# One stage of a two-block transformer kernel reordered: half-column inverse updates, branch tiles and preparation steps moved, beta and roots partly on ScalarE

## The chip, the cores and the metric

The program runs on one core of one Trainium2 chip. The metric is the device time of the whole program in microseconds. TensorE multiplies matrices into PSUM, VectorE and ScalarE work elementwise (ScalarE also evaluates functions), GpSimd (POOL) works elementwise on SBUF alone, and SyncE issues the loads.

## The reference

Two transformer blocks on 512 tokens of width 1024. The second block adds 16 meta tokens (528 tokens) and mixes them with two branches, a gated delta net and a stick-breaking attention. The change lies in the delta net:

```python
q = l2norm(heads(jax.nn.silu(causal_depthwise_conv(dq, conv_q)), DN_DK))
k = l2norm(heads(jax.nn.silu(causal_depthwise_conv(dk, conv_k)), DN_DK))
v = heads(jax.nn.silu(causal_depthwise_conv(dv, conv_v)), DN_DV)
g = -jnp.exp(a_log) * jax.nn.softplus(da + dt_bias)
beta = jax.nn.sigmoid(db)
...
decay = jnp.exp(jnp.where(incl, g[..., :, None] - g[..., None, :], -jnp.inf))
lower = jnp.where(strict, jnp.einsum('nbhid,nbhjd->nbhij', kb, k) * decay, 0.0)
sol = lax.linalg.triangular_solve(eye + lower, rhs, left_side=True, lower=True)
...
v_new = u_c - jnp.einsum('bhcd,bhde->bhce', w_c, S)
o = jnp.einsum('bhcd,bhde->bhce', qd_c, S) + jnp.einsum('bhij,bhje->bhie', attn_c, v_new)
S = S * gl_c[..., None, None] + jnp.einsum('bhcd,bhce->bhde', kd_c, v_new)
...
o_dn = rmsnorm_2(o_dn, dn_gain) * jax.nn.silu(heads(dz, DN_DV))
merged = jax.nn.sigmoid(gate_dn) * (o_dn @ w_branch_dn) + ...
```

There are 8 heads, keys of 128 and values of 256 channels.

## The kernel before, in words

**Tiles.** Activations lie with channels on partitions and tokens along the columns. Each weight product is taken in three parts for precision (`quantum`, line 950): high weights by high activations, high by low, low by high, as fp32r matmuls at L965. A unit is 128 output channels, 8 quanta (the eight 128-channel pieces of the input), so 24 matmuls of 512 columns or 48 of 264. ScalarE makes the high part of a unit's weights (w_hi), VectorE or GpSimd the low part (w_lo), some units ahead.

**The delta net's stage.** Its order is written out by hand. `delta_order` (line 106) builds one list, DELTA, and all engines walk it, each taking its own share of each event. The list has fills (w_proj quanta, "mm", and quanta of the output branch, "branch") and steps. `merged` (line 79) puts a step ahead of the fill whose index its number has reached; steps with equal numbers keep the order in which they were added, the preparation (PREPARE) ahead of the scan (SCAN). After an opening of 80 quanta (heads 0 and 1 are projected, head 0 is prepared) pass i does, at once:
- 48 quanta: q, k and the two v units of head i+2 (slots of 264 x 2 columns) and the two z units of head i+1 (512 columns);
- 8 branch tiles of head i-1 (L1345, 6 matmuls of 512 columns), one after every second quantum of a unit (`beside`); pass 0 has none;
- PREPARE for head i+1: `bcast` (broadcast of gate and beta), `decay`, `pair` (kk and kq products, L1224), `turn` (a transpose, L1233), then the six levels x1, u1, ... x6, u6 of the inverse of a 128x128 triangular block, with four blocks of 128 and one of 16 (WIDE);
- SCAN for head i: v (L1303), s (L1310 and L1318) and k (L1291) for five chunks;
- NORM for head i, then `parts`: times silu(z), split into oh and ol for the branch of the next pass;
- L2NORM for head i+2: silu, sum of squares (L1332), root, scale.

**Level u** (lines 1261 and 2514): TensorE multiplies a block UT by the level's Xm and its transpose by UT (L1275, L1282), over all 128 columns; VectorE subtracts the whole product from UT, though it is zero outside of the level's half blocks. An fp32 matmul stands in the trace as two records.

**Order inside an engine.** VectorE and ScalarE work strictly in the list's order. VectorE's share of `bcast` makes DT and ekd, its share of `decay` multiplies DT by the mask after ScalarE's exponentials and then reads gl from gB; `scan_s` (2537) writes the state S, for which TensorE's next k waits. A projected unit's bank is copied out by ScalarE (`projected`, 1765: craw for q, k and v, zz for z) at the event after the unit's last quantum, followed by the w_hi of a later unit; VectorE convolves craw in four `taps` (2459) over the next events.

**Banks.** `Banks` hands two double banks round to units and branch tiles and four single banks to the steps. A unit holds its bank over its 8 quanta; the next use waits for the reader.

**Roots.** `l2` (1862 on ScalarE, 2563 and 2568 on VectorE) takes exp(-ln(x)/2) on ScalarE and corrects it by one Newton step on VectorE, that reads the sum again from PSUM (`l2_v`). Beta is computed as 1/(1+exp(-x)) on ScalarE and VectorE (`betas`, 2445).

The lines that hold most of this order:

```python
        elif i < NH:
            fills = beside(units[0], branches[0:4], 2) + beside(units[1], branches[4:8], 2) \
                + products("w_proj", units[2:])
...
        if i + 1 < NH:
            steps += [(at, s, i + 1) for at, s in PREPARE]
        if i < NH:
            steps += [(at, s, i) for at, s in SCAN + NORM]
```

## Time and profile before

| | |
|---|---|
| time, median of 3 runs | 3069.69 us (3067.41 to 3073.24) |
| the profiled execution | 3069.01 us |
| its span, first to last instruction | 3067.2 us |
| mean granted TensorE clock | 0.977 |
| busy TensorE, VectorE, ScalarE, GpSimd | 2879.8, 1558.2, 1089.2, 509.2 us |
| instructions | 37371 |

The times agree within 0.2%. Busy times come from the profiled execution; an engine can be busy while nothing waits for it, and TensorE's matmuls are pipelined, so the start of one record to the start of the next tells more than a record's own length. The granted clock is a share of 2.4 GHz; 0.50 is the lower of its two levels, 1.2 GHz. The delta net's stage runs from about 1405 to 2215 us.

### The profile page before, as it was taken

What the parts mean: (1) busy time and instruction counts of PE and PEld (TensorE: products, weight loads), DVE (VectorE), ACT (ScalarE), POOL (GpSimd) and SP (SyncE); (2) the same over time, 40 slices, a digit from 0 to 9 for tenths busy, and PEclk for the clock granted to TensorE, in tenths of its full rate; (3) what the DMA queues carried; (4) which work ended last, traced back from release to release, by engine and by line L of the source; (5) the groups of instructions that cost most, each with busy time, mean ns of one, the idle gap of its engine ahead of it and who ended that gap; (6) DMA issues with size and microseconds to landing.
All of it is one profiled execution on the core that took longest, in us unless ns stands there. A gap on an engine that the chain in (4) does not pass through costs nothing.

```text
span 3067.2 us, 37371 instructions
## 1 busy us (share of the span) xinstructions
PE 2879.8 (94%) x14589; PEld 2275.5 (74%) x14589; DVE 1558.2 (51%) x2191; ACT 1089.2 (36%) x1605; POOL 509.2 (17%) x299
## 2 busy tenths in 40 slices
...
DMA packets 67375, 237.38 MB, mean 77 GB/s; under 512 B 7808, under 2 KB 7936, under 8 KB 66816
## 3 DMA queue, kind: packets, MB, share of 16 engines
...
q14 instruction: 58, 0.48, 0.0%
...
## 4 chain that ended last, share of the span: by engine, by line
PE 78%; DVE 12%; ACT 7%; issue 1%; DMA 1%; POOL 0%; DVEq 0%; ACTq 0%; SPq 0%; POOLq 0%
PE ps L965 53%; PE ps L1345 3%; PE ps L995 3%; PE ps L1146 2%; DVE vv L397 2%; PE ps L1115 2%; PE ps L1246 1%; PE ps L1133 1%; ACT w_hi L379 1%; PE ps L1441 1%; PE ps L1282 1%; PE ps L1275 1%; PE ps L1168 1%; DVE r L397 1%; DVE accs L386 1%
## 5 line engine op out<-in xcount | busy, mean ns | idle before, releaser
L965 PE MATMUL ps<-Nh,w_hi 128*128 128x512 f32 (+1 forms) x1808 | 673.9, 373 | 37.5 <-ACT zz L379 20.0
L965 PE MATMUL ps<-Nl,w_hi 128*128 128x512 f32 (+1 forms) x1808 | 634.9, 351 | 0.0
L965 PE MATMUL ps<-Nh,w_lo 128*128 128x512 f32 (+1 forms) x1808 | 632.2, 350 | 0.0
L379 ACT ACTIVATE w_hi<-w_raw 128x1024 fp32r<-128x1024 f32 (+1 forms) x352 | 368.1, 1046 | 611.8 <-PE ps L965 527.6
L386 POOL TENSOR_TENSOR w_lo<-w_raw,w_hi 128x1024 fp32r<-128x1024 f32 x127 | 308.2, 2427 | 859.8 <-ACT w_hi L379 855.1
L965 PEld LDWEIGHTS ps<-Nh,w_hi 128*128 128x128 f32 x1808 | 346.7, 192 | 101.5 <-issue 51.9
L386 DVE TENSOR_TENSOR w_lo<-w_raw,w_hi 128x1024 fp32r<-128x1024 f32 (+1 forms) x225 | 276.3, 1228 | 281.6 <-ACT w_hi L379 272.4
L965 PEld LDWEIGHTS ps<-Nl,w_hi 128*128 128x128 f32 x1808 | 347.0, 192 | 49.2 <-issue 4.6
L965 PEld LDWEIGHTS ps<-Nh,w_lo 128*128 128x128 f32 x1808 | 346.6, 192 | 44.4
L965 PE MATMUL ps<-x1h,w_hi 128*128 128x512 f32 (+1 forms) x784 | 275.3, 351 | 8.8 <-ACT x1h L379 5.1
L965 PE MATMUL ps<-x1l,w_hi 128*128 128x512 f32 (+1 forms) x784 | 268.3, 342 | 0.0
L965 PE MATMUL ps<-x1h,w_lo 128*128 128x512 f32 (+1 forms) x784 | 266.2, 340 | 0.0
L965 PEld LDWEIGHTS ps<-x1h,w_hi 128*128 128x128 f32 x784 | 148.3, 189 | 42.4 <-issue 19.9
L965 PEld LDWEIGHTS ps<-x1l,w_hi 128*128 128x128 f32 x784 | 148.6, 190 | 19.1 <-issue 2.4
L965 PEld LDWEIGHTS ps<-x1h,w_lo 128*128 128x128 f32 x784 | 148.8, 190 | 18.4
L386 POOL TENSOR_TENSOR f_t<-f_t,f_t 128x768 f32<-128x768 f32 (+1 forms) x14 | 25.0, 1786 | 674.9 <-ACT f_t L379 674.9
L965 PE MATMUL ps<-h1l,w_hi 128*128 128x512 f32 x352 | 118.5, 337 | 0.0
L965 PE MATMUL ps<-h1h,w_hi 128*128 128x512 f32 x352 | 118.2, 336 | 0.0
L965 PE MATMUL ps<-h1h,w_lo 128*128 128x512 f32 x352 | 117.6, 334 | 0.0
L386 DVE TENSOR_TENSOR f_t<-f_t,ps 128x768 f32<-128x768 f32 (+1 forms) x44 | 36.1, 822 | 147.7 <-PE ps L965 147.2
L379 ACT ACTIVATE f_t<-ps 128x768 f32<-128x768 f32 (+1 forms) x44 | 31.0, 705 | 195.0 <-PE ps L965 194.7
L386 DVE TENSOR_TENSOR UT<-UT,ps 128x512 f32<-128x512 f32 (+2 forms) x112 | 64.6, 577 | 45.0 <-PE ps L1275 29.7
...
## 6 DMA issues: line engine op xcount, KB each, us to landing
...
```

The costliest lines, as they stand in the source:

```text
L379: self.then_inc(self.e.activation(out, in_, func, **kw), sem)
L386: self.then_inc(self.e.tensor_tensor(out, a, b, op), sem)
L397: self.then_inc(self.e.scalar_tensor_tensor(out=out, in0=a, scalar=s, in1=b, op0=op0, op1=op1), sem)
L965: ins = e.matmul(out[:, 512 * j:512 * j + n], a[:, kk, :], x[:, kk, c0:c0 + n], start=k == 0 and p == 0, stop=k == nt - 1 and p == 2)
L995: ins = e.matmul(bank[0:2, 0:512], t.sc[:, 2 * k:2 * k + 2], a[:, i, :], start=k == 0, stop=k == KT - 1)
L1115: ins = e.matmul(out[:, c0:c0 + nn], t.qT[r0:r0 + 64, h // 2, qb * P:(qb + 1) * P], t.kT[r0:r0 + 64, h // 4, c0:c0 + nn], start=True, stop ...
L1133: ins = e.matmul(ps[:, 6, :], t.vp[:, i, 2 * (h // 4) + h % 2, :], t.PT[h % 2][:, i, :], start=h % 2 == 0 and i == 0, stop=h % 2 == 1 and ...
L1146: ins = e.matmul(out, a[:, k, :], x[:, k, 0:TX], start=k == 0 and p == 0, stop=k == KT - 1 and p == 2)
L1168: ins = e.matmul(out, a[:, kk, :], x[:, kk, :], start=i % 4 == 0 and p == 0, stop=i % 4 == 3 and p == 2)
L1246: ins = e.matmul(bank[0:n, c * n:(c + 1) * n], t.LM[lv % 2][0:n, c0 + c, 0:n], UT[0:n, 1, c0 + c, 0:n], start=True, stop=True)
L1275: ins = e.matmul(bank[0:n, (at + c) * n:(at + c + 1) * n], UT[0:n, 0, c0 + c, 0:n], t.Xm[0:n, c0 + c, 0:n], start=True, stop=True)
L1345: ins = e.matmul(out[:, 0:TX], a[:, 2 * (k % 4) + x, :], b[:, x, MS], start=x == 0 and p == 0, stop=x == 1 and p == 2)
```

## The change

The order: branch tiles stand beside the values' units instead of q's and k's in passes 1 to 5; PREPARE takes 2.5 slots a step instead of 2 (0.92 of that in pass 6), `decay` at 3 instead of 4; L2NORM begins at 22.2 instead of 32; norm's gains, the l2 steps ("st") and the split for the branch ("hiz") are events of their own. The work: level u on half the columns; beta as a Sigmoid on ScalarE, without VectorE's two steps and reciprocal; a root's second reading and its square (Identity, Square) on ScalarE; the ones of the gates' scan come from a constant.

```diff
-PREPARE = ((0, "bcast"), (4, "decay"), (7, "pair"), (9, "turn"), (12, "x1"), (14, "u1"), (16, "x2"), (18, "u2"),
-           (20, "x3"), (22, "u3"), (24, "x4"), (26, "u4"), (28, "x5"), (30, "u5"), (32, "x6"), (34, "u6"))
+PREPARE = ((0, "bcast"), (3, "decay"), (7, "pair"), (10, "turn"), (13, "x1"), (15.5, "u1"), (18, "x2"), (20.5, "u2"),
+           (23, "x3"), (25.5, "u3"), (28, "x4"), (30.5, "u4"), (33, "x5"), (35.5, "u5"), (38, "x6"), (40.5, "u6"))
 SCAN = ((1, "v0"), (3, "s0"), (5, "k1"), (8, "v1"), (10, "s1"), (11, "k2"), (13, "v2"), (15, "s2"), (17, "k3"),
         (19, "v3"), (21, "s3"), (23, "k4"), (25, "v4"), (27, "s4"))
-NORM = ((28, "nsq"), (30, "norm"))
-L2NORM = ((32, "siluqk"), (35, "l2q"), (35.1, "lnq"), (38, "stq"), (41, "l2k"), (41.1, "lnk"), (44, "stk"), (47, "siluv"))
+NORM = ((28.2, "nsq"), (29.5, "norm"), (31, "gain0"), (32, "gain1"))
+L2NORM = ((22.2, "siluqk"), (24.2, "l2q"), (24.3, "lnq"), (26.2, "stq0"), (27, "stq1"), (28, "stq2"),
+          (31.2, "l2k"), (31.3, "lnk"), (34, "stk0"), (35, "stk1"), (36, "stk2"), (46, "siluv"))
-FIRST_L2NORM = (((26, "siluqk"), (31, "l2q"), (31.1, "lnq"), (33, "stq"), (36, "l2k"), (36.1, "lnk"), (38, "stk"),
-                 (42, "siluv")),
+FIRST_L2NORM = (((26, "siluqk"), (30, "l2q"), (30.1, "lnq"), (33.5, "stq0"), (34.2, "stq1"), (35, "stq2"), (35.2, "l2k"),
+                 (35.3, "lnk"), (38, "stk0"), (39, "stk1"), (40, "stk2"), (41, "siluv")),
...
-FIRST_PREPARE = ((33, "bcast"), (38.5, "decay"), (46, "pair"), (49, "turn"), (52, "x1"), (54.5, "u1"), (57, "x2"),
...
+FIRST_PREPARE = ((32, "bcast"), (36, "decay"), (44, "pair"), (46.5, "turn"), (49, "x1"), (51.5, "u1"), (54, "x2"),
...
-    steps = [(13, "gates", 0), (21, "betas", 0), (31, "columns", 0)]
+    steps = [(13, "gates", 0), (30.2, "columns", 0)]
...
+        elif i + 2 < NH:
+            fills = products("w_proj", units[0:2]) + beside(units[2], branches[0:4], 2) \
+                + beside(units[3], branches[4:8], 2) + products("w_proj", units[4:])
...
-            steps += [(at, s, i + 1) for at, s in PREPARE]
+            steps += [(at * (1 if i + 2 < NH else 0.92), s, i + 1) for at, s in PREPARE]
...
-            steps += [(at, s, i) for at, s in L2NORM] + [(32.1, "siluz", i), (40, "parts", i)]
+            steps += [(at, s, i) for at, s in L2NORM] + [(22.3, "siluz", i), (41, "parts", i), (42.5, "hiz", i)]
         elif i < NH:
-            steps += [(35 if i == NH - 2 else 25.1, "siluz", i), (39 if i == NH - 2 else 36, "parts", i)]
+            steps += [(25.1, "siluz", i), (33, "parts", i), (34.5, "hiz", i)]
...
 (TensorE, level_u: the first product, then the second)
-                    ins = e.matmul(bank[0:n, (at + c) * n:(at + c + 1) * n], UT[0:n, 0, c0 + c, 0:n], t.Xm[0:n, c0 + c, 0:n],
+                    out = bank[0:n, (at + c) * half:(at + c + 1) * half].rearrange("k (p b) -> k p b", b=1 << lv)
+                    ins = e.matmul(out, UT[0:n, 0, c0 + c, 0:n], block_columns(t.Xm[0:n, c0 + c, 0:n], lv, 0),
...
-                ins = e.matmul(bank[0:n, c * n:(c + 1) * n], t.Xm[0:n, c0 + c, 0:n], UT[0:n, 0, c0 + c, 0:n],
+                out = bank[0:n, c * half:(c + 1) * half].rearrange("k (p b) -> k p b", b=1 << lv)
+                ins = e.matmul(out, t.Xm[0:n, c0 + c, 0:n], block_columns(UT[0:n, 0, c0 + c, 0:n], lv, 1),
...
 (VectorE, level_u)
+            first, second = (blocks(UT[0:n, x, c0:c0 + C, 0:n], lv, 1 - x) for x in (1, 0))
...
+                w.tt(first, first, packed(bank, lv, n, C), ALU.subtract, s.p_us)
...
+            w.tt(second, second, packed(bank, lv, n, C), ALU.subtract, s.p_us)
...
 (ScalarE, the opening)
+    w.act(as_halves(t.gbt[32:40, :], COLS2), halves(pair(ps, B.of["p", split_of("w_proj", 0)][0]), COLS2)[32:40],
+          ACT.Sigmoid, s.dg_act)
...
-    w.act(eb, eb, ACT.Exp, s.dg_act)
...
 (ScalarE, l2)
+            w.act(t.r[1][:, c0:c0 + n], src, ACT.Identity, s.l2_v, bias=cs("eps", n=1))
+        w.act(t.r[5][:], t.r[2][:], ACT.Exp, s.act_step, scale=-0.5)
+        w.act(t.r[2][:], t.r[5][:], ACT.Square, s.l2_exp)
         if i == 0:
             w.act(t.r[0][:], t.QK[h % 3][:, 1, :], ACT.Square, s.l2_sq)
-        w.act(t.r[5][:], t.r[2][:], ACT.Exp, s.l2_exp, scale=-0.5)
...
 (VectorE)
-    w.ts(as_halves(eb, COLS2), b[32:40], -1.0, None, ALU.mult, None, s.dg_dve)
-        w.memset(ea, 1.0, s.dg_dve)
-        w.ts(eb, eb, 1.0, None, ALU.add, None, s.dg_dve)
-        w.then_inc(e.reciprocal(t.gbt[32:40, :], eb), s.dg_dve)
...
-            w.ts(t.r[1][:, c0:c0 + n], ps[:, B.of[(*ev, j)][0], 0:n], 1.0, EPS, ALU.mult, ALU.add, s.l2_v)
-        w.tt(t.r[2][:], t.r[2][:], y, ALU.mult, s.step)
```

`block_columns` and `blocks` pick, of each pair of neighbouring blocks of 2^lv columns, the first or the second; `packed` reads the product, which lies without gaps in its bank. The bank of unit 0 is released by ScalarE's second gate step instead of VectorE's third.

## Rows read from the trace of the kernel before

**Rows 1.** The page, part 1: busy time of each engine.

```profile
PE 2879.8 (94%) x14589; PEld 2275.5 (74%) x14589; DVE 1558.2 (51%) x2191; ACT 1089.2 (36%) x1605; POOL 509.2 (17%) x299
```

**Rows 2.** Windows: stretch, length, busy PE, PEld, DVE, ACT, POOL, granted clock, DMA.

```profile
1405.00:1515.00 110.00, 87.86 (x609) 81.45 (x607) 89.30 (x116) 46.36 (x69) 43.14 (x26) 0.88 0.17 56
1515.00:1605.50 90.50, 82.55 (x560) 72.35 (x559) 53.78 (x82) 39.66 (x65) 31.36 (x21) 0.98 0.10 30
...
1793.60:1888.90 95.30, 86.99 (x561) 75.65 (x562) 63.74 (x89) 40.85 (x66) 35.90 (x23) 0.97 0.15 45
...
2080.10:2154.40 74.30, 72.44 (x453) 61.63 (x454) 37.04 (x61) 29.15 (x50) 30.34 (x21) 0.96 0.16 45
```

**Rows 3.** Timeline of PE, 1780 to 1815: start, us, instruction, [idle before].

```profile
1782.75 0.47 PE L965 MATMUL ps<-Nh,w_hi 128*128 128x512 f32 x1 [1.60 <-ACT craw L379]
1793.66 0.56 PE L965 MATMUL ps<-Nh,w_hi 128*128 128x264 f32 x1 [3.98 <-ACT zz L379]
1811.30 0.77 PE L1233 MATMUL ps<-const,UT 128*128 128x128 f32 x5 [1.23 <-DVE AT L386]
```

**Rows 4.** Timeline of ACT, 1776 to 1795.

```profile
1780.53 1.36 ACT L379 ACTIVATE oh<-O 128x512 fp32r<-128x512 f32 x2 [4.81 <-DVE O L386]
1791.74 1.08 ACT L379 ACTIVATE vv<-vv 128x1056 f32<-128x1056 f32 x1 [4.78 <-DVE vv L397]
```

**Rows 5.** Timeline of PE, 1750 to 1756 and 1056 to 1063.

```profile
1752.19 1.05 PE L1275 MATMUL ps<-Xm,UT 128*128 128x128 f32 x8
...
1753.89 0.37 PE L965 MATMUL ps<-Nh,w_hi 128*128 128x264 f32 x1
...
1754.71 0.29 PE L1317 MATMUL ps<-qk,S 128*128 128x16 f32 x2
...
1060.43 1.85 PE L1053 MATMUL ps<-acc_c,const 128*128 128x16 f32 x16
1062.13 0.47 PE L965 MATMUL ps<-Nh,w_hi 128*128 128x512 f32 x1
```

**Rows 6.** Groups by line and shape, 1400 to 2215: count | busy us, mean ns | idle.

```profile
L386 DVE TENSOR_TENSOR UT<-UT,ps 128x512 f32<-128x512 f32 x88 | 60.5, 688 | 42.5 <-PE ps L1275 29.7 <-PE ps L1282 9.2
L379 ACT ACTIVATE r<-ps,const 128x264 f32<-128x264 f32 x32 | 15.4, 481 | 5.5 <-DVE qk L397 3.3
L379 ACT ACTIVATE w_hi<-w_raw 128x1024 fp32r<-128x1024 f32 x69 | 73.1, 1059 | 9.9 <-PE ps L965 2.9 <-PE ps L1345 0.7
```

**Rows 7.** Timeline of pass 0's start, 1520 to 1537, PE, ACT and DVE.

```profile
1520.41 1.17 PE L1212 MATMUL ps<-gbt,const 8*128 8x264 f32 x8
1525.51 0.70 PE L1310 MATMUL ps<-V,kd 128*128 128x256 f32 x2 [1.12 <-ACT V L379]
1527.10 1.28 ACT L374 ACT_TABLE_LOAD   x1
1528.39 0.88 ACT L379 ACTIVATE DT<-DT 128x512 f32<-128x512 f32 x2
1529.77 0.64 ACT L379 ACTIVATE gB<-gB 128x528 f32<-128x528 f32 x1
1530.44 0.98 DVE L391 TENSOR_SCALAR gl<-gB 128x4 f32<-128x4 f32 x1 [0.25 <-ACT gB L379]
```

**Rows 8.** Waits of PE, 1400 to 2215: us in total, times, longest.

```profile
PE ps L1345 <- POOL ol L386: 6.9, 2, 5.8
```

**Rows 9.** Timeline of PE in the opening, 1428 to 1508, its longer waits.

```profile
1431.88 0.69 PE L1205 MATMUL ps<-const,gbt 40*128 40x40 f32 x5 [3.32 <-DVE gbt L2448]
...
1451.95 3.62 PE L1224 MATMUL ps<-qk 128*128 128x128 f32 x20 [2.65 <-DVE qk L397]
...
1461.57 1.05 PE L1233 MATMUL ps<-const,UT 128*128 128x128 f32 x4 [3.62 <-DVE UT L386]
1464.01 0.19 PE L1233 MATMUL ps<-const,UT 16*16 16x16 f32 x1 [1.38 <-DVE UT L386]
...
1507.66 0.55 PE L1246 MATMUL ps<-UT,LM 128*128 128x128 f32 x1 [6.98 <-DVE UT L386]
```

More of the change, by code:

```diff
@@ L923, in chunks, with blocks, block_columns, packed @@
     return ap[:, c0 * P:c0 * P + C * n].rearrange("p (a b) -> p a b", b=n)
+def blocks(ap, lv, second):
+    return ap.rearrange("k c (p t b) -> k c p t b", t=2, b=1 << lv)[:, :, :, second, :]
+def block_columns(ap, lv, second):
+    return ap.rearrange("k (p t b) -> k p t b", t=2, b=1 << lv)[:, :, second, :]
+def packed(ap, lv, n, C):
+    return ap[0:n, 0:C * n // 2].rearrange("k (c p b) -> k c p b", c=C, b=1 << lv)
 def each(ap, n, C):
@@ L1269, in level_u @@
             both = (2 << lv) < n
+            half = n // 2
             bank = ps[:, bank_of((f"u{lv}", h, j)), :]
@@ L1780, in scalar @@
     highs(split_of("w_proj", 1), last)
-    za, ea, la = (t.r[i][0:8, :] for i in range(3))
-    eb = t.r[3][32:40, :]
-    w.wait_ge(s.dg_dve, 3)
+    ea, la = (t.r[i][0:8, :] for i in (1, 2))
+    w.act(as_halves(t.gbt[32:40, :], COLS2), halves(pair(ps, B.of["p", split_of("w_proj", 0)][0]), COLS2)[32:40],
+          ACT.Sigmoid, s.dg_act)
+    w.wait_ge(s.dg_dve, 2)
     w.act(ea, ea, ACT.Exp, s.dg_act, scale=-1.0)
     w.act(la, ea, ACT.Ln, s.dg_act, bias=1.0)
-    w.act(eb, eb, ACT.Exp, s.dg_act)
     w.act(t.r[4][0:8, 0:1], sm("a_log", 0, 1, (0, 8)), ACT.Exp, s.dg_act)
@@ L1922, in scalar @@
             norm(h)
-        elif name == "parts":
+        elif name == "hiz":
             parts(h)
@@ L2442, in gates @@
             w.own()
[L2443 to L2448 removed]
+            w.then_inc(e.tensor_tensor_scan(t.gbt[0:8, cc], cs("ones")[0:8, 0:n], za[:, cc], 0.0, ALU.mult, ALU.add), s.dg_dve)
     def columns():
@@ L2518, in level_u @@
             both = (2 << lv) < n
-            if i == 1 and both:
-                w.wait_ge(s.p_um, 14 * h + US[lv - 1] + j + 1)
-                a = UT[0:n, :, c0:c0 + C, 0:n]
-                d = ps[0:n, B.of[f"u{lv}", h, j][0], 0:2 * C * n].rearrange("p (x a b) -> p x a b", x=2, b=n)
-                w.tt(a, a, d, ALU.subtract, s.p_us)
-                continue
-            for x in (1, 0) if both else (0,):
-                w.wait_ge(s.p_um, 14 * h + US[lv - 1] + j + 1)
-                a = UT[0:n, x, c0:c0 + C, 0:n]
-                w.tt(a, a, in_chunks(ps[:, B.of[f"u{lv}", h, j][0], :], n, C), ALU.subtract, s.p_us)
+            first, second = (blocks(UT[0:n, x, c0:c0 + C, 0:n], lv, 1 - x) for x in (1, 0))
+            w.wait_ge(s.p_um, 14 * h + US[lv - 1] + j + 1)
+            bank = ps[:, B.of[f"u{lv}", h, j][0], :]
+            j += 1
+            if both and i == 1:
+                w.tt(first, first, packed(bank[:, C * n // 2:C * n], lv, n, C), ALU.subtract, s.step)
+            elif both:
+                w.tt(first, first, packed(bank, lv, n, C), ALU.subtract, s.p_us)
+                w.wait_ge(s.p_um, 14 * h + US[lv - 1] + j + 1)
+                bank = ps[:, B.of[f"u{lv}", h, j][0], :]
                 j += 1
+            w.tt(second, second, packed(bank, lv, n, C), ALU.subtract, s.p_us)
     def scan_k(h, c):
@@ L2554, in norm, with gain @@
         w.stt(y, qf, 1.5, y, ALU.add, ALU.mult, s.n_step)
-        for x in range(2):
-            w.stt(O[:, x, :], O[:, x, :], sm("dn_gain", x), y, ALU.mult, ALU.mult, s.n_step)
+    def gain(h, x):
+        O = t.O[h % 2][:, x, MS]
+        w.stt(O, O, sm("dn_gain", x), t.r[4][:, MS], ALU.mult, ALU.mult, s.n_step)
     def parts(h):
```

49 lines of the change are left out of this document (21 added, 28 removed), and 2 rows, old and new, of the table FIRST_L2NORM.

## The prediction

> **What bounds the kernel now.** The page comes first: TensorE is busy 94% of the span [rows 1]. So a microsecond is won where TensorE waits, or where its own work gets shorter. The change touches only the delta net's stage, so the second view cuts that stage at its passes, one head to a pass [rows 2]. In each row the reader subtracts TensorE's busy time from the stretch: 22.1 us idle in the opening (1405 to 1515), 8.0 in pass 0, 8.3 in pass 3 (passes 1, 2, 4, 5 show 8.2, 8.1, 8.2, 8.6 in rows of the same kind), and 1.9 in pass 6. The granted clock is the second loss: 0.88 in the opening costs 110 x 0.12 = 13.2 us, 0.98 in pass 0 1.8, 0.97 in pass 3 2.9; passes 1 to 6 lose about 17 together. A middle pass therefore gives away 8.3 + 2.9 = 11.2 us of 95.
>
> The third view names a pass's waits [rows 3]: 1.60 for craw, 3.98 for zz, 1.23 for AT; the rest of the 8.3, 1.5, stands before the l2 products, for the squares. The fall of the clock follows the 3.98. The fourth says why [rows 4]: ScalarE is no bottleneck, but it works in program order. It stood 4.81 us before the oh copies and 4.78 before the values' silu, both for VectorE, and behind them queued the copies that free TensorE's two product banks.
>
> **The change part by part.**
>
> *Half columns on TensorE.* 704 records of 128 columns become 64. What matters is the spacing: 16 records of 128 columns take 1753.89 - 1752.19 = 1.70 us, and 16 records of another product, also on 128x128 weights but with 16 moving columns, take 1062.13 - 1060.43 = 1.70 [rows 5]. The same 0.106 us, so the columns do not set it. I take 0. The bound on the other side is half the spacing, 704 x 0.053 = 37 us.
>
> A rule of the Trainium skill speaks against this reading: "TensorE: Matmul & The Clock Gate", section "Back-to-back issue gap", gives an isolated gap that shrinks with the columns down to a floor of about 60 cycles; by it the sum would be some 37 us lower. Section "LDWEIGHTS (loading the stationary operand)" of the same page gives columns / 1.2, 107 ns for 128, which is what the rows show.
>
> *Half columns on VectorE.* 88 updates of 688 ns [rows 6] shrink to somewhere between 0.34 and 0.48 us each, about 20 us of its work. The l2 steps lose one product and two reads of PSUM per root. All this lies beside TensorE; it counts only where TensorE waits for VectorE, that is, in the opening and behind rows 4. If strided access cost the full 688 ns, the passes would still have room (VectorE is busy 63.7 of 95.3 us).
>
> *The copies before oh and silu.* "hiz" goes to 42.5, behind the craw copy of the unit that ended before slot 40, and the k steps leave slots 41 to 47 for 31 to 36. The 1.60 and the 3.98 go, and so does the squares' 1.5, since silu and l2 start ten slots sooner. That is 7.1 of 8.3. What is late next has to be read from the new order.
>
> *Slots 0 to 3 without a branch.* Pass 0 has no branches today, so it shows what such a start costs [rows 7]. From bcast at 1520.41 the scan's first product stands 1.12 us for V, until 5.1 us after bcast, since ScalarE first makes four bcast copies, zz and w_hi. New in every pass: 1.1.
>
> *decay at 3.* This ties with s0, and the preparation is listed first, so VectorE's mask and gl come ahead of the S copy, and both wait for ScalarE's exponentials. From V at 5.1: the table 1.28, then DT to gB's end 2.02 (1528.39 to 1530.41), near 8.4; gl, which took 0.98 beside GpSimd [rows 7], ends near 9.4; S, at an estimated 0.4 with its hand-over, makes 9.9. k1 would be there at 5.1 + 0.9 + two tiles of 0.8 (1753.89 to 1754.71 [rows 5]) = 7.6. New wait: 2.3. The later LT and turn then find VectorE ready, so the AT wait falls from 1.23 to 0.3.
>
> *The roots on ScalarE.* Each l2 gets two Identity passes and a Square more, and "lnq" at 24.3 stands ahead of v4 at 25. From l2q's first matmul V needs 0.6 + 1.28 table + 4 x 0.48 [rows 6] + 3 x 0.64 + 0.4 = 6.1 us, and TensorE reaches s4 after l2q 0.9, v4 0.5, a tile 0.8, u3 1.8 and a tile 0.8 = 4.8 (estimates from the counts of matmuls and rows 5). New wait: 1.4, between 0 and 2.6.
>
> *The branch's w_hi.* Branch 3 now ends before slot 28, so its w_hi of 1.06 [rows 6] comes between x4 and the squares of "nsq", as does that of the third unit. Norm's product then waits between 0 and 2.4; I take 1.1. Small bank waits: 0.4.
>
> A pass then idles 1.1 + 2.3 + 0.3 + 1.4 + 1.1 + 0.4 = 6.6 instead of 8.3. Over passes 1 to 5: 41.4 - 33 = -8.4. The clock: the old wait of 3.98 costs 2.9; pass 0, whose 8.0 are spread over many small waits, lost 1.8. I take 2 per pass, 12 for 17: -5. Pass 6 gets the decay wait without losing one of 3.98: +1.5. Pass 0 has no branch: 8.0 to 6.0, -2. Of the two waits for ol [rows 8] pass 7's, 6.9 - 5.8 = 1.1, goes, since parts is earlier: -1; the last, 5.8, is a chain of data and stays.
>
> *Opening.* The wait for columns, 3.32 behind the reciprocal [rows 9], goes with beta on ScalarE, but l2q now sits a slot before it and waits for silu and square, which the taps of k hold back: I find the same place passed at nearly the same time, gain 0. The sigmoid costs ScalarE 0.6 us and two table loads of 1.28, in a time when it waits for VectorE anyway; if it did not, the bank of unit 0 would hold TensorE up to 3 us. VectorE has an estimated 5 us less from beta and 3 less from q and k, and the pair is taken before the last taps: of the pair's 2.65 and the turn's 3.62 and 1.38, 2.6 stay, -5. The wait of 6.98 for u5 shrinks to about 2, -5. Clock 13.2 to about 8, -5. Together -15, between -4 and -27.
>
> The sum: -8.4 - 5 + 1.5 - 2 - 1 - 15 = -30 us. The profiled execution took 3069.0 (span 3067.2 and 1.8 around it), within 0.7 of the median of 3069.7. That gives 3039.
>
> **The rivals.** A measurement of this kernel can tell about 0.2%, 6 us, from no change.
> - *The waits all vanish.* If ScalarE keeps ahead everywhere and only V's 1.1 stays: passes -36, their clock -15, pass 0 -8, pass 7 -1, opening -15: 2994. For it: ScalarE is busy 41 of 95 us. Against it: order, not load, made today's waits. 0.12.
> - *TensorE's spacing follows the columns* (the page's isolated gap): 3039 - 37 = 3002. Against it: rows 5. 0.05.
> - *Gain and loss cancel*: the opening gives 5 and the new waits take a pass's 11.2. 3063 to 3075, 0.07.
> - *Slower: ScalarE's longer order lets the clock fall twice a pass.* The place is k1 behind decay and s4 behind lnq. With waits at their upper bounds a pass idles 10, and each of two falls costs 2.9: 15.8 for 11.2. Passes +8.6 + 17.7, pass 6 +3, pass 0 +3, opening -4, pass 7 -1: +27, 3096. It decides from 11.2 us of idle and clock together in a pass. For it: the opening, with waits of 2.65 to 6.98 [rows 9], has the clock at 0.88, so waits not much longer than 2.3 cost a fall. Against it: pass 0, with 8.0 us idle, lost only 1.8. 0.16.
>
> **How the numbers follow.** My forecast, 3012 to 3062, has 0.60. Faster: 0.60 + 0.12 + 0.05 = 0.77; same 0.07; slower 0.16. The forecast's own range is 3012 to 3062; to leave out no more than 2 in 10 it reaches to 2995 (most of the first two rivals) and to 3080 (the start of the last).
>
> **What would show it.** Right: no wait for craw or zz on TensorE's products in passes 1 to 5; a wait of about 1 us for V at s0 and about 2.3 for S at k1 in passes 0 to 6; one for V at s4; the updates' 16 records still at 1.70 us; VectorE's busy time down by about 50 us and ScalarE's up by about 25. Wrong: k1 without a wait (S is not behind decay); 16 records in 0.9 us; a granted clock under 0.96 in the middle passes.

## The result: 24 us slower, and the profile after

The median went from 3068.55 us (3066.02 to 3073.24) to 3092.93 us (3089.01 to 3096.37), four runs each: ratio 1.0077, 95% interval 1.006 to 1.0095. The forecast was 3039, range 2995 to 3080: wrong in sign and outside its range. The profiled execution took 3096.4, its span is 3094.5.

The page of the changed kernel, part 1, against [rows 1]: VectorE has 52 us less work, ScalarE 32 more, TensorE 18 more with the same number of products (its mean clock is 0.971 for 0.977, and 0.006 of the span is 18 us).

```profile
PE 2897.4 (94%) x14589; PEld 2292.6 (74%) x14589; DVE 1506.2 (49%) x2155; ACT 1121.6 (36%) x1657; POOL 511.9 (17%) x299
```

To compare passes, both stages are now cut at bcast, the first step of a pass (in the kernel before 5.4 us behind the first cut of [rows 2], 5 to 6 us ahead of the others). Windows of the kernel before, opening, pass 0 and pass 3, columns as in [rows 2]:

```profile
1405.00:1520.40 115.40, 93.26 (x639) 85.91 (x637) 90.60 (x118) 46.96 (x70) 43.14 (x26) 0.88 0.16 53
1520.40:1600.00 79.60, 74.34 (x514) 65.97 (x513) 47.38 (x75) 34.00 (x58) 27.83 (x20) 0.98 0.12 34
1788.50:1883.70 95.20, 86.96 (x562) 75.63 (x561) 63.69 (x90) 40.81 (x65) 35.90 (x23) 0.96 0.15 44
```

The same stretches of the changed kernel:

```profile
1405.00:1518.40 113.40, 96.42 (x654) 89.90 (x652) 78.41 (x107) 57.27 (x85) 43.61 (x26) 0.88 0.18 54
1518.40:1605.50 87.10, 76.47 (x514) 66.32 (x513) 44.62 (x77) 41.98 (x69) 30.97 (x21) 0.96 0.09 31
1800.90:1900.30 99.40, 88.86 (x563) 77.31 (x563) 58.45 (x85) 44.06 (x72) 36.26 (x23) 0.95 0.14 43
```

The opening gives 2.0 us, pass 0 costs 7.5, pass 1 2.5, passes 2 to 5 together 16.5, and all behind them 2.8: 27.3, the difference of the two spans. The cut at 1405 hides something: the stage's first product after a wait of 6.18 us, which both kernels share, starts at 1394.99 before and at 1397.31 after, so 2.3 us are lost ahead of the stage, in work that is the same (run 1, with that work too, has 1394.45). Counted from that product the opening gives 4.3 us. In pass 3 TensorE idles 10.5 us instead of 8.2. What it waits for stands in the waits of PE, 1400 to 2241 (us in total, times, longest):

```profile
PE ps L1316 <- issue: 26.4, 7, 4.4
PE ps L1350 <- ACT qk L384: 8.1, 6, 2.0
PE ps L1245 <- DVE qk L402: 7.9, 1, 7.9
PE ps L1335 <- ACT V L384: 7.1, 5, 1.6
PE ps L1342 <- ACT V L384: 6.4, 5, 1.3
```

L1316 is the scan's k product, L1350 norm's, L1245 the opening's pair, L1335 and L1342 the scan's s. The waits for craw, zz and AT [rows 3] and for the squares are gone in passes 1 to 5. The new ones cost clock as well. Windows of 3 us around k1 and s4 of pass 3:

```profile
1813.00:1816.00 3.00, 1.73 (x6) 1.59 (x7) 1.51 (x3) 0.10 (x1) 0.79 (x2) 0.62 0.00 0
...
1858.00:1861.00 3.00, 2.62 (x9) 2.48 (x10) 0.67 (x1) 0.60 (x3) 0.00 (x0) 0.52 0.02 5
1861.00:1864.00 3.00, 3.00 (x10) 2.42 (x10) 0.00 (x0) 1.59 (x2) 1.24 (x1) 0.50 0.00 0
```

The granted clock falls towards its lower level, 1.2 GHz, twice a pass: behind k1 and at s4, where before it fell once, behind zz. The missing clock over a pass's 3 us windows (each window's length times one minus its granted clock) sums to 5.1 to 6.8 us in passes 1 to 5, where it was 3.4 in passes 2 to 5 and 1.7 in pass 1. In pass 3 k1's fall takes 1.7 of it and s4's 3.4.

Timeline of the changed kernel (start, us, engine, instruction, [idle before]): start of pass 1, start of pass 3, then later places of pass 3:

```profile
1607.32 1.25 DVE L398 TENSOR_SCALAR DT<-gB,gcol 128x128 f32<-128x128 f32 x4 [4.97 <-ACT gB L384]
...
1609.07 0.15 DVE L391 TENSOR_TENSOR ekd<-gB,gcol 16x1 f32<-16x1 f32 x1
...
1615.58 1.02 PE L1316 MATMUL ps<-S,qk 128*128 128x256 f32 x2 [2.36 <-issue]
...
1803.09 2.38 POOL L391 TENSOR_TENSOR w_lo<-w_raw,w_hi 128x1024 fp32r<-128x1024 f32 x1 [4.41 <-ACT w_hi L384]
1804.04 2.48 DVE L398 TENSOR_SCALAR DT<-gB,gcol 128x128 f32<-128x128 f32 x4 [3.98 <-ACT gB L384]
...
1806.89 2.37 POOL L391 TENSOR_TENSOR w_lo<-w_raw,w_hi 128x1024 fp32r<-128x1024 f32 x1 [1.42 <-ACT w_hi L384]
...
1807.01 2.25 DVE L391 TENSOR_TENSOR ekd<-gB,gcol 16x1 f32<-16x1 f32 x1
1809.29 1.28 ACT L379 ACT_TABLE_LOAD   x1 [2.00 <-DVE ekd L391]
1811.49 0.89 DVE L391 TENSOR_TENSOR DT<-DT,const 128x512 f32<-128x512 f32 x2 [2.23 <-ACT DT L384]
1812.64 0.97 DVE L396 TENSOR_SCALAR gl<-gB 128x4 f32<-128x4 f32 x1 [0.26 <-ACT gB L384]
1813.74 0.42 DVE L396 TENSOR_SCALAR S<-ps 128x256 f32<-128x256 f32 x1
1814.27 1.19 PE L1316 MATMUL ps<-S,qk 128*128 128x256 f32 x2 [4.34 <-issue]
...
1858.38 0.61 PE L1342 MATMUL ps<-qk,S 128*128 128x16 f32 x2 [1.27 <-ACT V L384]
...
1871.52 1.00 PE L1299 MATMUL ps<-Xm,UT 128*128 128x64 f32 x8
1872.35 1.06 PE L1307 MATMUL ps<-UT,Xm 128*128 128x64 f32 x8
1873.22 0.37 PE L985 MATMUL ps<-Nh,w_hi 128*128 128x264 f32 x1
```

k1 waits for the S copy at 1813.74, which stands behind the mask and gl of decay, and these behind ScalarE's table and exponentials, and these behind ekd. In pass 1 that is 2.36 us, as forecast (2.3). In passes 2 to 5 it is 4.3 and in pass 6 4.4, since DT and ekd take 2.48 and 2.25 us there instead of 1.25 and 0.15: GpSimd makes one w_lo beside DT and another beside ekd. In passes 0 and 1 no w_lo lies beside them.

### The profile page after: what moved, and what is told of

Same layout as the page of the kernel before. It is cut to its first block, busy times and chain, and to the rows that moved or that the text cites. A ratio compares the mean times of both kernels' runs of the same rounds, so it can differ in the third digit from the quotient of the medians.

```text
span 3094.5 us, 37380 instructions
## 1 busy us (share of the span) xinstructions
PE 2897.4 (94%) x14589; PEld 2292.6 (74%) x14589; DVE 1506.2 (49%) x2155; ACT 1121.6 (36%) x1657; POOL 511.9 (17%) x299
## 4 chain that ended last, share of the span: by engine, by line
PE 78%; DVE 10%; ACT 7%; issue 2%; POOL 1%; DMA 1%; DVEq 0%; ACTq 0%; SPq 0%; POOLq 0%
PE ps L985 53%; PE ps L1370 3%; PE ps L1015 2%; PE ps L1166 2%; PE ps L1135 2%; ACT w_hi L384 2%; PE ps L1267 1%; DVE vv L402 1%; PE ps L1153 1%; PE ps L1188 1%; ACT r L384 1%; PE ps L1466 1%; PE ps L1307 1%; DVE accs L391 1%; PE ps L1299 1%
## 5 line engine op out<-in xcount | busy, mean ns | idle before, releaser
L391 POOL TENSOR_TENSOR LM<-LT,const 128x512 f32<-128x512 f32 (+1 forms) x72 | 79.4, 1103 | 23.9 <-DVE LT L391 13.9
```

What stands on the lines that cost most here:

```text
L391: self.then_inc(self.e.tensor_tensor(out, a, b, op), sem)
```

## Experiments

| | median us | to the kernel before, 95% | the theory's time |
|---|---|---|---|
| 1 decay behind s0 | 3060.67 | 0.9987 (0.9977, 0.9996) | held |
| 2 root behind v4 | 3093.26 | 1.009 (1.0075, 1.0105) | missed, 3070 |
| 3 both | 3069.92 | 1.0013 (1.0002, 1.0024) | missed, 3030 to 3045 |
| 4 whole columns | 3096.51 | 1.01 (1.0083, 1.0117) | held |
| 5 run 1, pass 0's roots later | 3058.91 | 0.9969 (0.9958, 0.9979) | missed, 3053 to 3056 |
| 6 run 1, squares and root moved | 3077.71 | 1.0033 (1.0021, 1.0045) | missed, 3036 to 3048 |
| 7 run 1, opening's roots closed up | 3060.9 | 0.9978 (0.9969, 0.9988) | missed, 3055 to 3058 |
| 8 before, decay at 3 | 3094.87 | 1.0088 (1.0075, 1.0102) | held |
| 9 run 5, squares moved | 3063.41 | 0.9992 (0.9983, 1.0001) | missed, 3047 to 3053 |
| 10 changed work, old step numbers | 3042.7 | 0.9923 (0.9911, 0.9936) | missed, 3056 to 3068 |
| 11 run 1, branches first | 3077.97 | 1.0039 (1.0026, 1.0052) | missed, 3048 to 3058 |
| 12 run 5, whole columns | 3067.8 | 1.0005 (0.9996, 1.0013) | 0.8 us over |
| 13 run 10, Square of k first | 3045.86 | 0.9927 (0.9914, 0.9939) | missed, 3028 to 3036 |
| 14 run 13, spread preparation | 3030.84 | 0.9876 (0.9863, 0.989) | missed, slower by 2 to 10 |
| 15 run 10, whole columns | 3043.96 | 0.9923 (0.991, 0.9935) | slower by less than its 4 to 9 |
| 16 run 10, old roots | 3051.18 | 0.9944 (0.993, 0.9958) | slower by less than its 12 to 22 |
| 17 run 14, pass 0 not spread | 3029.28 | 0.9876 (0.9863, 0.989) | missed, 3024 to 3027 |
| 18 run 14, branches beside values | 3054.86 | 0.9961 (0.9947, 0.9974) | slower by more than its 12 to 20 |

**The tie of decay and s0.** Run 1 takes it out of the changed kernel, run 8 puts it alone into the kernel before.

```diff
-PREPARE = ((0, "bcast"), (3, "decay"), ...       run 1
+PREPARE = ((0, "bcast"), (3.5, "decay"), ...
-PREPARE = ((0, "bcast"), (4, "decay"), ...       run 8, in the kernel before
+PREPARE = ((0, "bcast"), (3, "decay"), ...
```

> The changed kernel with decay at 3.5 instead of 3, so that VectorE copies S (s0) ahead of the mask and gl. Theory (k1 waits for S, which stands behind decay's mask and gl on VectorE): k1's waits (26.4 us over seven passes, 4.3 in most) go, and with them the clock's fall behind k1 (1.7 to 3.4 us a pass); the time falls by 30 to 45 us, to 3050 to 3063. Rival 1 (k1 waits for the scaled k of GpSimd or for a bank, not for S): k1 still waits over 3 us and the time stays within 6 us of 3093. Rival 2 (TensorE only meets the same wait at the pair, which needs nothing of S but comes behind the same work on VectorE): k1's wait goes, one at pair or turn takes its place, and the time falls by under 15 us.

> The kernel before with one number changed: decay at 3 instead of 4, so that it is listed ahead of s0, as in the change. Theory (this tie alone makes the wait at k1, whatever the rest of the change does): k1 waits 2.3 to 4.4 us in passes 0 to 6 and the clock falls behind it; slower by 20 to 35 us, 3086 to 3100. Rival (in the kernel before TensorE still waits for zz just ahead of this place, so that a wait at k1 only takes over part of it, and the branch tiles of slots 0 to 3 cover the rest): slower by under 8 us.

Run 1 is 32 us faster than the change by the medians and 28 by the ratios, run 8 27 us slower than before. Window and timeline of run 8's pass 3:

```profile
1800.20:1899.20 99.00, 87.78 (x563) 76.11 (x562) 63.73 (x90) 40.80 (x65) 35.90 (x23) 0.95 0.14 44
```

```profile
1817.63 1.19 PE L1291 MATMUL ps<-S,qk 128*128 128x256 f32 x2 [4.00 <-issue]
```

The wait at k1 is there, 4.0 us, and the pass is 99.0 long instead of 95.2, though zz and craw still cost what they did. One number of the list makes a loss as large as the whole one, in either kernel. Shown.

**The second fall, at s4.** Run 2 puts ScalarE's root of q behind the copy of V; run 3 does both.

```diff
-... (24.2, "l2q"), (24.3, "lnq"), ...
+... (24.2, "l2q"), (25.1, "lnq"), ...
```

> The changed kernel with lnq at 25.1 instead of 24.3, so that ScalarE copies V of the last chunk ahead of the root of q. Theory (s4's wait of 1.27 us stands behind the root, and with the thin products behind it brings the second fall of the clock in a pass): the wait for V at s4 goes, the granted clock at s4 no longer falls to 0.5, and the time falls by 5 x (1.3 + 3.4) = 23 us, to about 3070. Rival (the clock falls there for the thin products themselves, and the wait only adds its own length): the wait goes, the clock still falls at s4, and the time falls by 5 to 8 us. Second rival: stq0 on VectorE is now late and holds the taps, and the wait moves to norm's squares: no change.

> Both edits together: decay at 3.5 and lnq at 25.1. Theory (two separate losses of a pass, each with its own fall of the clock): the gains of the two runs add up within 6 us, to 3030 to 3045, which is faster than the kernel before. Rival (one loss hides the other, since TensorE is caught up by ScalarE at the next wait): the gain is no more than the larger of the two plus 5 us.

Run 2 changes nothing. V's wait is gone, and at u3 just ahead of it TensorE stands nearly as long for the bank that the unread sum of q holds. Timeline of run 2:

```profile
1857.68 1.29 PE L1307 MATMUL ps<-UT,Xm 128*128 128x64 f32 x10 [1.00 <-ACT r L384]
```

The clock still falls there (0.79, 0.50, 0.57 from 1858 on). So another owner of the wait changes nothing, and whether the clock falls there for the wait or for the thin products around it stays open. Run 3 is slower than run 1: theory wrong. It waits 6.8 us for that bank where run 1 waits 6.3 for V, and its missing clock does not follow the waits: 5.1 us in pass 2 with 6.8 us idle, none in pass 4 with 8.4. Why the clock falls in one pass and not in the next is open.

**The rest of the changed order.** Runs 5, 6, 7, 9 and 11 each move something of run 1.

```diff
+steps += [(at + (8 if i == 0 and at < 40 else 0), s, i) for at, s in L2NORM] ...    run 5
-NORM = ((28.2, "nsq"), ...
+NORM = ((27.1, "nsq"), ...                                                          runs 6 and 9
-(24.2, "l2q"), (24.3, "lnq"), (26.2, "stq0"), (27, "stq1"), (28, "stq2")
+(25.6, "l2q"), (25.7, "lnq"), (28, "stq0"), (28.9, "stq1"), (30, "stq2")            run 6
-(33.5, "stq0"), (34.2, "stq1"), (35, "stq2"), ... (38, "stk0"), (39, "stk1"), (40, "stk2")
+(33.5, "stq0"), (33.6, "stq1"), (33.7, "stq2"), ... (38, "stk0"), (38.1, "stk1"), (38.2, "stk2")  run 7
-fills = products("w_proj", units[0:2]) + beside(units[2], ...) + beside(units[3], ...) ...
+fills = beside(units[0], ...) + beside(units[1], ...) + products("w_proj", units[2:])   run 11
+steps += [(at + (8 if at < 40 else 0), s, i) for at, s in L2NORM] ...               run 11, siluz too
```

> The first run's kernel (decay at 3.5), and in pass 0 the steps from siluqk to stk2 eight slots later (silu at 30.2 instead of 22.2). Theory (pass 0 has no branch tiles between the taps of k and the silu, so l2q waits 4.46 us for silu and square, norm's squares wait behind the roots for 1.95, and the clock falls there): both waits shrink under 1.5 us together, pass 0 goes from 88 to 80 to 83 us, and the time from 3060.7 to 3053 to 3056. Rival (pass 0 is long for another reason, the thinner spread of the preparation, and the wait reappears later in the same pass): within 3 us of 3060.7.

> The first run's kernel, with nsq at 27.1 (right behind s4, ahead of the third unit's copies and w_hi on ScalarE) and the sum and root of q both behind v4 and u3 (l2q at 25.6, lnq at 25.7). Theory (V at s4, 1.26 us, waits behind the root, the norm product, 1.3 us, behind two w_hi; moving the whole of l2q leaves no bank held as in the second run): both waits go in passes 0 to 5, 2.5 us a pass, and with them some of the clock's falls of 1.7 to 3.4 us: 3060.7 minus 13 to 25, 3036 to 3048. Rival (ScalarE's work is only shifted, and what was V's wait becomes one for Xm, craw or a bank within ten slots, as in the second run): within 6 us of 3060.7.

> The first run's kernel, with the three VectorE steps of each root of head 0 back to back in the opening (stq 33.5, 33.6, 33.7; stk 38, 38.1, 38.2) instead of spread between the taps of v. Theory (the pair waits 5.9 us because the scaling of k stands behind taps of v that the spreading put between its steps, and ScalarE's root of k behind the scaling of q): the pair's wait falls to 1 to 3 us, the time by 3 to 6, to 3055 to 3058. Rival (the taps put behind hold up the next unit's bank): a wait for craw of 2 us or more appears before the pair, and the time stays within 3 us.

> The fifth run's kernel (decay at 3.5, pass 0's roots eight slots later) with nsq alone moved, from 28.2 to 27.1, and the roots left where the change put them. Theory (in the sixth run it was the later root that hurt, through VectorE, where the update of u4 stood 4.1 us behind it; the squares themselves only wait for two w_hi): norm's wait of 1.3 us goes, no wait of 4 us stands before x5; 3058.9 minus 6 to 12, 3047 to 3053. Rival (the squares ahead hold up craw, Xm and the banks behind them): a wait for craw of 1.4 us stays and the time is within 4 us of 3058.9 or above.

> The first run's kernel (decay at 3.5) with the branch tiles beside units 0 and 1 again, as before the change, and the roots eight slots later in every pass, which that needs. Theory (without a branch in slots 0 to 3 TensorE meets V at s0 too early, 1.6 us a pass; with one it does not, and the craw and zz waits stay away thanks to hiz and the closer k steps): the wait for V at s0 goes in passes 1 to 5 and craw and zz don't come back; 3056 to 3060.7 minus 8, so 3048 to 3058. Rival (the branch's tiles are what covered the roots; beside the first units their cover is lost, and siluv or zz waits return): 3062 or more.

Run 5: pass 0 is 82.4 us instead of 88.4, and the wait of 4.46 for l2q is down to 2.61 (norm's squares keep theirs, 2.00), but the total gives only 2 us (6 by the ratios): the mechanism holds, its price is unclear at this spread (run 1's times lie between 3057.2 and 3069.2). Runs 6 and 9: the 1.3 us at norm go in run 9 and fall to 0.68 in run 6, and the update before x5 comes late (up to 4.7 us in run 6, which also waits 1.4 for craw, and 3.1 in run 9). PE's timeline of run 6, then of run 11:

```profile
1863.96 2.05 PE L1267 MATMUL ps<-UT,LM 128*128 128x128 f32 x8 [4.69 <-DVE UT L391]
```

```profile
1863.76 1.97 PE L1299 MATMUL ps<-Xm,UT 128*128 128x64 f32 x8 [4.71 <-ACT Xm L384]
```

In run 11 V's wait at s0 is gone as well, for this one and 1.8 for zz. In all three the place of a wait was right and its removal made another. That the serving engine has no free place in its order there, though it has free time in sum, is argued from this and not shown by itself. Run 7: the pair still waits 7.78 us (5.90 in run 1, 7.94 in the change); no change, theory wrong.

**The work by itself.** Run 4 and 12 take the half columns out of the changed order with and without the tie; run 10 puts the changed work at the step numbers of the kernel before; 15 and 16 take half columns and roots out of that; 13 moves one Square.

```diff
-ins = e.matmul(out, t.Xm[...], block_columns(UT[0:n, 0, c0 + c, 0:n], lv, 1), ...)      4, 12, 15
+ins = e.matmul(bank[0:n, c * n:(c + 1) * n], t.Xm[...], UT[0:n, 0, c0 + c, 0:n], ...)
-w.act(t.r[1][:, c0:c0 + n], src, ACT.Identity, s.l2_v, ...)                             16
-w.act(t.r[2][:], t.r[5][:], ACT.Square, s.l2_exp)
+w.ts(t.r[1][:, c0:c0 + n], ps[...], 1.0, EPS, ALU.mult, ALU.add, s.l2_v)   (VectorE)
+w.tt(tt, tt, y, ALU.mult, s.step)                                         (VectorE)
+if i == 0: w.act(t.r[0][:], t.QK[h % 3][:, 1, :], ACT.Square, s.l2_sq)                  13
 w.act(t.r[5][:], t.r[2][:], ACT.Exp, s.act_step, scale=-0.5)
 w.act(t.r[2][:], t.r[5][:], ACT.Square, s.l2_exp)
-if i == 0: w.act(t.r[0][:], t.QK[h % 3][:, 1, :], ACT.Square, s.l2_sq)
```

> The changed kernel with level u of the kernel before: whole products of 128 columns and whole subtractions. Theory (TensorE's spacing is set by the weights, and VectorE's half columns lie beside TensorE): 16 update records take 1.70 us with either, VectorE's busy time rises by about 25 us, the time stays within 6 us of 3093. Rival 1 (half columns do save time on TensorE or shorten the chain of the inverse): slower by 10 us or more. Rival 2 (the strided columns cost more than they save, and are part of the loss): faster by 6 us or more.

> The fifth run's kernel with level u on whole columns, as in the kernel before. Theory (half columns buy no TensorE time; they only shorten VectorE's chain before each x level by 0.2 to 0.3 us per subtraction): 16 records still 1.70 us, the UT waits before x levels up by under 1 us a pass; slower than the fifth run by 2 to 8 us, 3061 to 3067. Rival 1 (half columns matter once k1 no longer waits): slower by over 8 us. Rival 2 (no part in the time at all): within 2 us.

> The changed kernel's work (half columns, beta as a sigmoid, Identity and Square of the roots on ScalarE, split parts and gains) in the order of the kernel before: all step numbers, branch places and first steps as there. Theory (order makes the loss, work is nearly free): k1 without a wait, craw and zz waits of 1.6 and 4.0 are back, VectorE's busy time is down by 50 us, and the time is that of the kernel before or up to 10 us less: 3056 to 3068. Rival (the work itself costs, by more ScalarE ahead of the copies TensorE needs): 3072 or more, with new waits for ACT behind the roots.

> The tenth run's kernel with whole columns in level u, as before the change: what is left of the work is beta and the roots. Theory (the roots' work, about 4.5 us of VectorE between slots 35 and 47, took away zz and craw; half columns only shorten chains by 0.3 us each): slower than 3042.7 by 4 to 9 us, no wait for zz of over 1 us. Rival (the half columns' 5 to 6 us of VectorE a pass were what freed craw and zz): slower by 15 us or more, with a wait for zz of 3 us or more.

> The tenth run's kernel with the roots as before the change (VectorE reads the sum from PSUM and forms the square): what is left of the work is half columns and beta. Theory (the roots are what freed craw and zz): waits for craw and zz of together 4 us or more in passes 1 to 5, with a fall of the clock; slower than 3042.7 by 12 to 22 us, 3055 to 3065. Rival (half columns did it): at most 6 us slower, and the wait of 2.88 us for the square of k gone. Second rival (both are needed): a zz wait of 1 to 3 us, and 6 to 12 us slower.

> The tenth run's kernel (the changed work in the old order) with the Square of k on ScalarE ahead of the root's Exp and Square again, as in the kernel before. Theory (the 2.88 us wait at the sum of k stands behind Exp and Square, 2 x 0.66 us, and the Square of k itself): the wait falls by 1.3 us to about 1.6 in passes 1 to 5 and some of the clock's falls there go; 3042.7 minus 7 to 15, 3028 to 3036. Rival (VectorE then gets the root 0.65 us later and zz or craw, which the tenth run has only just lost, come back): within 4 us of 3042.7 or above.

Run 10 is the surprise: 3042.7, 23 us faster than before. But its order is not quite that of the kernel before. The steps that the change had split off have numbers of their own, and `merged` puts a step at 40.01 one fill behind a step at 40:

```diff
-NORM = ((28, "nsq"), (30, "norm"))                                    in the kernel before
+NORM = ((28, "nsq"), (30, "norm"), (30.01, "gain0"), (30.02, "gain1"))
-... (38, "stq"), ... (44, "stk"), ...
+... (38, "stq0"), (38.01, "stq1"), (38.02, "stq2"), ... (44, "stk0"), (44.01, "stk1"), (44.02, "stk2"), ...
-... (40, "parts", i)
+... (40, "parts", i), (40.01, "hiz", i)
```

So gains, the last two steps of each root and hiz come a slot later than in the kernel before, and hiz with it behind the craw copy, as in the change. This holds for runs 13 to 18 too. Run 10's window of pass 3, and its timeline around it:

```profile
1781.10:1872.40 91.30, 86.03 (x562) 74.41 (x561) 60.28 (x85) 44.04 (x72) 37.35 (x23) 0.98 0.15 47
```

```profile
1768.05 0.61 ACT L383 ACTIVATE craw<-ps 128x528 f32<-128x528 f32 x1
...
1770.32 0.63 ACT L383 ACTIVATE oh<-O 128x512 fp32r<-128x512 f32 x1 [0.51 <-DVE O L390]
...
1859.30 1.16 PE L1356 MATMUL ps<-r,const 128*128 128x264 f32 x4 [2.88 <-ACT r L383]
...
1870.17 1.09 ACT L383 ACTIVATE vv<-vv 128x1056 f32<-128x1056 f32 x1 [0.22 <-DVE vv L401]
1871.35 0.60 ACT L383 ACTIVATE zz<-ps 128x512 f32<-128x512 f32 x1
```

The craw copy stands ahead of oh, where it stood behind it and its wait of 4.81 [rows 4], and craw's wait is gone. ScalarE waits 0.22 us for vv where it waited 4.78 [rows 4], so zz is out in time as well: VectorE has less to do between slot 35 and 47. The 2.88 is new: the Square of k stands behind the root. Run 16, with the roots as before, has zz back, run 15 has not, and neither has craw back; run 13 brings the 2.88 down to 1.53 and gets a zz wait for it. Timeline of run 16, then of run 13:

```profile
1782.52 0.56 PE L984 MATMUL ps<-Nh,w_hi 128*128 128x264 f32 x1 [3.79 <-ACT zz L383]
```

```profile
1782.35 0.56 PE L984 MATMUL ps<-Nh,w_hi 128*128 128x264 f32 x1 [2.06 <-ACT zz L383]
```

So the roots freed zz. They are worth 0.2% there, 6 to 9 us, half columns nothing (both ratios 0.9923). That leaves 15 to 17 of run 10's 23 us to what runs 15 and 16 share: beta, and the steps that come a slot later. Passes 1 to 5 take 461.8 us in run 10 and 460.7 in run 16, where the kernel before takes 475.0; of these 13 to 14 us, 8 are craw's wait, 1.6 in each pass. It went with hiz behind the craw copy in three runs out of three, but no run puts hiz back, and none takes roots and half columns out together. In the changed order half columns are worth 0.4% (run 12 against 5), and 0.2% with the tie (run 4, intervals overlap), a little more than the expectation of run 12 had.

**The order, piece by piece, on that work.**

```diff
-PREPARE = ((0, "bcast"), (4, "decay"), (7, "pair"), (9, "turn"), ...                    14
+PREPARE = ((0, "bcast"), (3.5, "decay"), (7, "pair"), (10, "turn"), (13, "x1"), (15.5, "u1"), ...
+... for at, s in (PREPARE if i else PREPARE_0)      17; PREPARE_0 is that of the kernel before
-fills = beside(units[0], ...) + beside(units[1], ...) + products("w_proj", units[2:])    18
+fills = products("w_proj", units[0:2]) + beside(units[2], ...) + beside(units[3], ...) ...
```

> The thirteenth run's kernel with the changed PREPARE alone (2.5 slots a step, 0.92 of it in pass 6), decay at 3.5. Theory (spreading takes the AT wait of 1.2 us at turn away, but puts u5, x6 and u6 into the place where VectorE works off taps, roots and parts, so UT waits and a wait for craw or zz come there): 2 to 10 us slower than the thirteenth. Rival (the spread is what the change gains by, and the branches' and roots' new places are what costs): faster than the thirteenth by 3 us or more.

> The fourteenth run's kernel with the preparation in pass 0 spaced as before the change (2 slots a step, decay at 4), spread in passes 1 to 6 only. Theory (pass 0 is short, without branch tiles, so the spread puts x5 behind VectorE's taps and roots, a wait of 5.3 us, and a fall of the clock): pass 0 goes from 85.0 back to 79.4 us and the time from 3030.8 to 3024 to 3027. Rival (head 1 prepared earlier only moves the wait on to pass 1): within 2 us.

> The fourteenth run's kernel with the branch tiles of passes 1 to 5 beside the values' units, as in the change; roots, norm and parts stay at the old slots. Theory (slots 0 to 3 without a branch uncover V at s0, 1.6 us, and S at k2, 0.85, as in the first run): about 2.5 us more idle time in each of five passes and one fall of the clock in some, 12 to 20 us slower, 3043 to 3051; so the branches' place is over half of the 28 us. Rival (the earlier roots and norm are what cost, by V at s4 and the squares): slower by under 6 us. Second rival (the branch tiles cover the values' taps, which is worth as much as it costs): faster.

The spread gains 15 us, against the theory. Windows of run 14 (passes 0, 1, 3), of run 17 (pass 1), and of run 18 (pass 3):

```profile
1514.30:1599.30 85.00, 75.92 (x514) 67.10 (x513) 46.88 (x77) 41.56 (x69) 31.87 (x21) 0.96 0.10 32
1599.30:1686.50 87.20, 84.06 (x562) 73.60 (x561) 59.86 (x85) 43.66 (x72) 34.49 (x23) 1.00 0.15 49
1775.60:1864.40 88.80, 85.68 (x563) 75.16 (x563) 58.35 (x85) 44.05 (x72) 37.48 (x23) 0.98 0.15 48
```

```profile
1596.80:1690.50 93.70, 86.50 (x562) 75.69 (x562) 63.02 (x89) 49.03 (x78) 36.97 (x24) 0.96 0.14 46
```

```profile
1784.20:1878.30 94.10, 86.65 (x562) 75.81 (x561) 58.23 (x85) 44.10 (x72) 36.78 (x23) 0.96 0.14 46
```

In run 14 TensorE idles 3.1 us in pass 3. Run 17 gets pass 0 back to 79.4 and pays it in pass 1, 93.7 for 87.2: the rival. Run 18 costs 24 us: V at s0 waits 1.13, S at k2 0.86, and one wait grows from 1.9 to 4.9. The timelines of run 14, then run 18, at that place:

```profile
1836.43 0.69 DVE L390 TENSOR_TENSOR qk<-qk,r 128x512 f32<-128x512 f32 x1
1837.89 1.54 DVE L401 SCALAR_TENSOR_TENSOR O<-O,small,r 128x512 f32<-128x512 f32 x2
1839.53 0.95 DVE L390 TENSOR_TENSOR UT<-UT,ps 128x256 f32<-128x256 f32 x2
1840.05 1.28 PE L1266 MATMUL ps<-UT,LM 128*128 128x128 f32 x7 [1.92 <-issue]
```

```profile
1844.02 1.59 POOL L390 TENSOR_TENSOR qk<-qk,gB 128x528 f32<-128x528 f32 x1
1844.46 1.70 DVE L390 TENSOR_TENSOR qk<-qk,r 128x512 f32<-128x512 f32 x1
1845.75 1.53 POOL L390 TENSOR_TENSOR LM<-LT,const 128x512 f32<-128x512 f32 x1
1846.20 1.64 DVE L401 SCALAR_TENSOR_TENSOR r<-qk,r 128x512 f32<-128x512 f32 x1
1850.32 0.94 DVE L390 TENSOR_TENSOR UT<-UT,ps 128x256 f32<-128x256 f32 x2
1850.84 1.41 PE L1266 MATMUL ps<-UT,LM 128*128 128x128 f32 x5 [4.93 <-issue]
```

The update stands behind norm on VectorE in both; in run 18 three of norm's steps meet GpSimd's and take 1.6 to 1.7 us instead of 0.7, and a tap of v (0.77) comes between. Runs 14 and 17 beat both kernels: 0.9876, 37 to 39 us under the kernel before.

## Why the prediction was wrong

The step that failed is the price of the new waits. The sum took a middle pass from 8.3 us idle to 6.6 and its missing clock to 2; pass 3 idles 10.5 and misses 5.1. The runs put most of it down to one wait, k1's for S: without it (run 1) passes 1 to 5 idle 38.3 us instead of 48.0 and miss 6.8 us of clock instead of 27.2. Priced at 2.3 us and no fall, it cost 27 to 32 us.

The forecast of -30 and the difference of 27.3 between the two profiled executions lie 57 us apart. They split so: idle time of passes 1 to 5 +8 where -8.4 was forecast, their clock +12 for -5, the opening -4.3 for -15, pass 0 +7.5 for -2, all behind pass 5 +2.8 for +0.5, and 2.3 that lie ahead of the stage. No single term turned the sign.

The account that the runs give, in medians (by the ratios in brackets): changed work, with hiz, gains and late root steps a slot behind, -23 (-24, run 10); spread -15 (14 against 13, which equals 10 within its interval); branches beside the values +24 (+26, 18 against 14); earlier roots, norm and parts with the changed opening and the Square of k behind the root +6 (+8, 1 against 18; +4 and +2 with pass 0's roots later, run 5); the tie +32 (+28, the change against 1).

By its own steps:
- **Half columns, on TensorE 0:** right. From 1871.52 over 1872.35 to 1873.22, 16 records with 64 columns take 1.70 us, as with 128 [rows 5]. The rival of a spacing that follows the columns falls. Its 37 us was half the measured spacing times 704, not worked out from the cycles of the gap that it names.
- **Half columns, on VectorE 0.34 to 0.48 us each:** right, the form's mean is 0.421; VectorE -52 (forecast -50), ScalarE +32 (25).
- **craw, zz and squares go, 7.1 of 8.3:** they went. For craw's 1.6 the step's reason, hiz behind the copy, fits runs 10, 15 and 16. For zz's 4.0 it gave the k steps' slots and the earlier silu; runs 10 and 16 show that VectorE's lighter root does it at the old numbers. The text had noted that VectorE's work counts behind [rows 4], and then credited only the order. Whether the changed order would free zz with the old roots is not tested.
- **V at s0 1.1; V at s4 1.4; norm 1.1:** 1.13 in passes 0 and 1 and 1.6 in passes 3 to 5; 1.27 in passes 1 to 5; 1.0 to 1.3, and 1.96 in pass 0. Right.
- **S at k1 2.3:** right in place, and in size in passes 0 and 1 (2.33, 2.36); 4.3 in passes 2 to 5 and 4.40 in pass 6. The durations came from pass 0 [rows 7], where GpSimd makes no w_lo beside DT and ekd. This term was mis-sized, by 2.0.
- **Idle 6.6 a pass:** 10.5 in pass 3. Beyond k1's 2.0, waits for the branch's sum (0.77), UT (0.5) and gB (0.6) were not forecast.
- **Clock 2 a pass:** 5.1 to 6.8, the other mis-sized term. The 2 was taken from pass 0, read as 8.0 us idle in small waits without a fall. But pass 0 had one: the clock stands at its lower level behind the wait of 1.81 at turn, which is all of its 1.8 (row below). A wait of 2.3 could have been priced with a fall from that. Run 1 takes out k1's wait, and the idle time of pass 3 falls by 2.7 and the missing clock from 5.1 to 1.7.

```profile
1537.00:1540.00 3.00, 3.00 (x12) 2.82 (x13) 0.00 (x0) 2.29 (x4) 0.36 (x1) 0.50 0.00 0
```

- **Pass 0 -2:** +7.5. A pass without branch tiles was taken as unaffected, but its silu came at 22.2 behind taps of k that GpSimd's LM stretched: waits of 4.46 for l2q and 1.96 for norm's squares.
- **Opening -15:** -4.3 from the shared product on. u5's 6.98 went (-5 was forecast). Its clock, where -5 was forecast, did not change: 0.88 and 0.88. The columns' place came out even, as forecast: the 3.32 went, and what came for it hangs on the execution. The first wait for craw is 5.2 us in the change and l2q then waits 0.59; in run 1, with the same opening, it is 2.4 and l2q waits 4.20 (before: 2.4). Runs 8 and 17 wait 5.2 for craw as well, and in them and in the change the stage starts over 2 us later, which no edit explains. The pair's 2.65 became 7.94, and with turn's two waits 9.7 for 7.65, where 5 had been struck out: VectorE's three root steps are spread among taps, and closing them up (run 7) did not help. Why is open.
- **ol 5.8 stays, 1.15 goes:** right.

The slower rival (3096, chance 0.16) had the mechanism: k1 behind decay, s4 behind the root, two falls of the clock a pass. For k1 runs 1 and 8 show it; for s4 run 2 shows the fall but not that the root's place makes it. That its number lies 3 us off is in part luck: it had 26 us in the passes where its own 15.8 for 11.2 gives 23 and the traces 19, and 3 in pass 0 for 7.5. What was argued against it, that pass 0 lost only 1.8 us of clock with 8 idle, overlooked that this 1.8 was a fall, and that pass 0's own longest wait, 2.70, stood at its end, so that its fall was counted to pass 1.
